# The second layer's adaLN weights summed on VectorE during the merge

## The chip, the cores and the metric

One core of a Trainium2 chip runs the whole program in one launch. The metric is the device time of an execution in microseconds. The engines are TensorE (matmuls, PE in the profile), VectorE (DVE), ScalarE (ACT), GpSimd (POOL) and SyncE (SP), which here only issues DMAs.

## What is computed

A block with a three-branch token mixer and an expert layer is followed by two transformer layers. Before each layer a conditioning vector makes the six modulation vectors (adaLN), and the change is about these:

```python
# first block (D_MODEL = 1024, SEQ = 256)
mod_l = jnp.split((jax.nn.silu(c) @ ada_w[l] + ada_b[l])[:, None, :], 6, axis=-1)
mod_c = jnp.split((jax.nn.silu(c_ctx) @ ada_w[l] + ada_b[l])[None, None, :], 6, axis=-1)
zc = modulate(rmsnorm(ctx, norm1_w[l]), mod_c[0], mod_c[1]) @ w_in[l] + b_in[l]
zl = modulate(rmsnorm(x, norm1_w[l]), mod_l[0], mod_l[1]) @ w_in[l] + b_in[l]
ml_c, st_f, st_b = mlstm_branch(zc[...], ...)       # context first, its state goes on
ml_l, _, _ = mlstm_branch(zl[...], ..., st_f, st_b)
x = x + mod_l[2] * token_mixer_out(zl, lat_grid, lp, ml_l)   # hyena, fnet, mLSTM, gated and merged
x = x + mod_l[5] * hier_moe(modulate(rmsnorm(x, norm2_w[l]), mod_l[3], mod_l[4]), lp)
...
# second block, for each of two layers
mod = jnp.einsum('bd,dn->bn', c_act, w_ada[layer]) + b_ada[layer]
sh1, sc1, gt1, sh2, sc2, gt2 = jnp.split(mod, 6, axis=-1)
```

Each modulation is a vector of 1024 times a matrix of 1024 by 6144, in float32. The kernel calls 512 columns of such a matrix a unit (2.10 MB): `ada0` is the first block's matrix, `ada1` that of the second block's first layer, `ada2` that of its second.

## The kernel before

**Stages.** The first 280 us project the input in ten passes (`PASSES`: q, k, kc, v, vc, o, vh, x1, x2, fn; kc and vc are the context's). A pass (`in_pass`) is four pieces of TensorE work on one weight unit, and between the pieces stand other jobs: the Hyena filters, the spectra, from pass 5 on the mLSTM's gates, and in passes 6 to 9 the heads. Head j needs, in turn, TensorE's row maximum, VectorE's weight arguments, ScalarE's exponential, VectorE's products and TensorE's values, and then `head_out` on VectorE, which frees the bank for the next head. The merge follows (280 to 457 us): twelve steps of gates and branch product on TensorE, sigmoid on ScalarE, `merge` on VectorE, with the Fourier and Hyena branches between them. Then come the output projection, the turn of x2 (normalised rows transposed), the router and the expert stage.

**Where the adaLN work stands.** 24 units, `ada0` 0 to 11 and `ada1` 0 to 11, are numbered 0 to 23. The first four are done ahead of the passes. Each pass has two of the other twenty, a after piece 0 and b after piece 2. A unit goes one of two ways. TensorE adds it to a bank with the 8 instructions of `strip_rows` (16 records in the trace, shape 20x512). Or, for those in `SUMMED` (10 to 14, 17, 19), VectorE's `ada_sum` multiplies and adds its eight blocks in place and `strip_columns` turns the row of sums with 16 one-column products. The last strip unit, 23 in pass 9, closes the bank: ScalarE copies it (`strip_in`) and `strip_columns` turns it.

**What sets the order.** Every engine's instructions are in written order. Weights pass through one ring of 18432 columns, cut in four quads during the passes and in three slots from the merge on. `unit_order` lists the loads and the releases, `unit_plan` gives each load its place and the release that it waits for. SP issues the loads in list order, and a load that waits holds all those behind it. `SUMS_BEFORE` names the loads that also wait for a count of VectorE's sums.

**Names for the prediction.** `norm_of_filters` is TensorE's first use of the context's hT, in pass 1. The wait at the end of pass 5 is that of `gate_columns`. In the merge `hyena_products(o)` on VectorE stands between `hyena_spectrum(o)` and `hyena_inverse(o)` on TensorE. `gates_of(n)` needs merge unit n // 2: gates 4 need unit 2, gates 10 unit 5.

## Time and profile before

| | us |
|---|---|
| median of 3 timed runs | 1922.56 (1921.06 to 1926.6) |
| the profiled execution | 1927.68 |
| its span | 1925.8 |
| TensorE busy | 1842.1, 96% |
| VectorE busy | 688.6, 36% |
| ScalarE busy | 312.8, 16% |
| mean granted TensorE clock | 0.989 of full |

The span runs from the first to the last instruction. Busy shares are means over the program. "idle before" in a row is the time for which an engine stood still ahead of it, with the engine that ended the wait; "records" are the lines that the trace has for an instruction (a float32 matmul of full rows leaves two).

### The profile page before, as it was taken

How to read it: one execution, taken by the hardware profiler on the slowest of the kernel's cores; microseconds unless marked ns; L12 is line 12 of the kernel's file. 1: busy time of each engine (PE TensorE's matmuls, PEld its weight loads, DVE VectorE, ACT ScalarE, POOL GpSimd, SP SyncE). 2: the span in 40 equal slices, each digit the busy share in tenths (PEclk: the TensorE clock that was granted, in tenths of full speed). 3: DMA queues.
4: the chain of work that ended last, by engine and by line, in shares of the span. 5: the costliest groups of instructions: out<-in, count | busy, mean ns of one | idle time of the engine just before them, and what ended most of it. 6: DMA issues, size and time to landing. Idle time of an engine off the chain costs nothing.

```text
span 1925.8 us, 39004 instructions
## 1 busy us (share of the span) xinstructions
PE 1842.1 (96%) x17396; PEld 1080.7 (56%) x17396; DVE 688.6 (36%) x1670; ACT 312.8 (16%) x729; POOL 26.5 (1%) x41
## 2 busy tenths in 40 slices
PE   6999989999898899999999999999999999999997
PEld 2654767886777555577676555443444444343444
DVE  3766772622433665432323553311110111111023
ACT  3211121001233324200001242100000010000001
POOL 0100000000000000000000000100000000000000
PEclk9999999999999999999999999999999999999999
DMA  9967743353699443467675323799999999999995
GB/s 359 341 244 272 272 153 118 131 178 119 263 401 388 164 141 123 148 235 256 236 242 190 131 91 128 294 402 420 409 419 409 416 409 405 420 412 415 410 413 217
DMA packets 156047, 538.84 MB, mean 280 GB/s; under 512 B 10016, under 2 KB 34944, under 8 KB 121712
## 3 DMA queue, kind: packets, MB, share of 16 engines
q1 hardware_dynamic: 149360, 509.15, 68.7%
q0 software_dynamic: 3728, 17.58, 2.6%
q10 hardware_dynamic: 2784, 9.53, 1.3%
q8 instruction: 140, 2.29, 0.5%
q14 instruction: 35, 0.29, 0.0%
HBM read 527.18 MB, written 12.19 MB: 280 GB/s over the span
## 4 chain that ended last, share of the span: by engine, by line
PE 87%; DVE 6%; DMA 2%; issue 1%; DVEq 1%; ACT 1%; SPq 0%; POOL 0%; ACTq 0%; POOLq 0%
PE ps L1279 24%; PE ps L1315 12%; PE ps L1225 8%; PE ps L1513 8%; PE ps L1089 4%; PE ps L1207 4%; PE ps L1237 4%; PE ps L892 4%; PE ps L1291 3%; PE ps L1104 2%; PE ps L1333 2%; PE ps L757 2%; PE ps L699 1%; PE ps L1302 1%; DMA ring<-in_ada_w 1%
## 5 line engine op out<-in xcount | busy, mean ns | idle before, releaser
L1279 PE MATMUL ps<-ring,arena 128*32 128x512 f32 (+1 forms) x4608 | 459.1, 557 | 0.0
L1279 PEld LDWEIGHTS ps<-ring,arena 128*32 128x32 f32 x4608 | 148.9, 110 | 294.0 <-issue 288.2
L1315 PE MATMUL ps<-ring,arena 128*32 128x256 f32 x4224 | 232.2, 379 | 0.1
L1315 PEld LDWEIGHTS ps<-ring,arena 128*32 128x32 f32 x4224 | 139.4, 110 | 96.9 <-issue 12.4
L2862 DVE TENSOR_TENSOR arena<-arena,ps 128x256 f32<-128x256 f32 (+1 forms) x72 | 27.0, 375 | 390.8 <-ACT arena L1965 390.8
L1513 PE MATMUL ps<-ring,hT 128*128 128x512 f32 (+1 forms) x384 | 154.9, 554 | 1.1 <-DVE hT L2214 1.1
L1225 PE MATMUL ps<-hT,ring 128*128 128x256 f32 x704 | 153.8, 379 | 0.7 <-DVE hT L2214 0.7
L1225 PEld LDWEIGHTS ps<-hT,ring 128*128 128x128 f32 x704 | 133.6, 190 | 23.4 <-issue 5.7
L1513 PEld LDWEIGHTS ps<-ring,hT 128*128 128x128 f32 x384 | 69.1, 190 | 68.7 <-issue 66.8
L2758 DVE TENSOR_SCALAR arena<-ps,ga,mod 128x128 f32<-128x128 f32 (+1 forms) x64 | 20.8, 389 | 197.5 <-PE ps L1330 118.1
L1089 PE MATMUL ps<-hT,ring 128*128 128x256 f32 x384 | 86.6, 385 | 3.9 <-DMA ring<-in_w_branch 3.9
L1965 ACT ACTIVATE arena<-ps 128x256 f32<-128x256 f32 (+1 forms) x72 | 21.2, 367 | 421.9 <-PE ps L1279 421.9
L892 PE MATMUL ps<-hT,ring 128*128 128x256 f32 x384 | 88.1, 383 | 0.8 <-DVE hT L2214 0.8
L1089 PEld LDWEIGHTS ps<-hT,ring 128*128 128x128 f32 x384 | 73.8, 193 | 14.6 <-DMA ring<-in_w_branch 4.3
L892 PEld LDWEIGHTS ps<-hT,ring 128*128 128x128 f32 x384 | 71.5, 190 | 17.6 <-issue 6.6
L1237 PE MATMUL ps<-ring,arena 128*128 128x512 f32 x176 | 78.4, 596 | 0.0
L1291 PE MATMUL ps<-ring,arena 128*32 128x128 f32 x2048 | 61.9, 276 | 10.5 <-issue 10.2
L2184 DVE SCALAR_TENSOR_TENSOR arena<-ring,cact,arena 128x512 f32<-128x512 f32 x84 | 63.1, 751 | 6.6 <-issue 0.4
L1291 PEld LDWEIGHTS ps<-ring,arena 128*32 128x32 f32 x2048 | 57.3, 111 | 14.2 <-issue 11.8
L2292 DVE SCALAR_TENSOR_TENSOR grow<-arena,colv,grow 128x189 f32<-128x189 f32 (+2 forms) x160 | 62.1, 430 | 6.3 <-issue 0.4
L2705 DVE TENSOR_TENSOR arena<-arena,ps 128x256 f32<-128x256 f32 x22 | 9.3, 421 | 145.8 <-ACT arena L1907 145.8
L1923 ACT ACTIVATE arena<-ps,mod,ga 128x128 f32<-128x128 f32 (+1 forms) x64 | 23.2, 443 | 226.5 <-PE ps L1330 130.9
(426 smaller groups left out, 1805.8 us busy)
## 6 DMA issues: line engine op xcount, KB each, us to landing
ring<-in_gate_up SPq DMA_DIRECT2D x160, 1024.0 KB, 14.2
ring<-in_down SPq DMA_DIRECT2D x104, 1024.0 KB, 15.2
ring<-in_gate_up_last SPq DMA_DIRECT2D x64, 768.0 KB, 13.9
ring<-in_w_ada SPq DMA_DIRECT2D x48, 768.0 KB, 6.1
ring<-in_w_in SPq DMA_DIRECT2D x36, 768.0 KB, 7.8
ring<-in_ada_w SPq DMA_DIRECT2D x24, 768.0 KB, 7.8
ring<-in_w_ada SPq DMA_DIRECT2D x24, 512.0 KB, 7.1
ring<-in_w_in SPq DMA_DIRECT2D x12, 1024.0 KB, 7.5
```

The lines of the kernel that those rows point to most:

```text
L757: last = mm(ps[32 * g:32 * g + rows, 2, :], cstrip[:, k, at:at + rows], quads[:, s, k * 512:(k + 1) * 512], start=r == 0 and i <= 4, stop= ...
L892: last = mm(ps[:, half, (i % 2) * T:(i % 2 + 1) * T], quads[:, s, k * 512 + i * P:k * 512 + (i + 1) * P], src[:, k, :], start=k == 0, stop ...
L1089: last = mm(ps[:, 2 * (n % 2), i * T:(i + 1) * T], w512(s, k, m * P, P), hT[:, k, :], start=k == 0, stop=k == KD - 1)
L1207: last = mm(ps[:, 2 * b + half, :], src[:, k, b * P:(b + 1) * P], w512(slots_[half], k), start=k == 0, stop=k == KD - 1)
L1225: m_ = mm(ps[:, hb, i * cols:(i + 1) * cols], ring[:, s, o:o + P], src[:, k, :], start=k == 0, stop=k == KD - 1)
L1237: m_ = mm(ps[:, base + 2 * b + half, :], region(R_AT, 2, T)[:, hb, b * P:(b + 1) * P], ring[:, s, o:o + 512], start=first and hb == 0, sto ...
L1279: last = mm(ps[32 * q:32 * q + 32, base + t_, 0:2 * n], src[:, k, 32 * t_:32 * t_ + 32], w[:, q], start=k == 0, stop=k == KD - 1)
L1291: last = mm(ps[32 * q:32 * q + 32, bank, t_ * P:(t_ + 1) * P], src[:, k, 32 * t_:32 * t_ + 32], w[:, t_ // 2, q], start=k == 0 and t_ == 0 ...
L1315: last = mm(ps[32 * q:32 * q + 32, bank + t_ // 2, (t_ % 2) * 256:(t_ % 2 + 1) * 256], rows[:, t_, o:o + 32], cells[:, cell, r * D + q * 2 ...
L1513: last = mm(ps[:, b, 0:w], hT[:, k, b * P:(b + 1) * P], w512(entry[0], k, 0, w, w), start=k == 0, stop=k == KD - 1)
L2184: last = v.scalar_tensor_tensor(acc, w, cact[:, c + k:c + k + 1], acc, ALU.mult, ALU.add)
L2292: v.scalar_tensor_tensor(acc[:, a, ro, co], grids[a][:, ri, ci], tap(b, (dr + 1) * 3 + dc + 1), acc[:, a, ro, co], ALU.mult, ALU.add)
```

## The change

Eight units of `ada1` (15, 16, 18 to 23, `MOVED`) leave the passes. Their loads go into slot 2 of the ring during the merge, one after another, each waiting for the sum of the one before. VectorE sums them into the arena at eight places of the merge. The merge units use slots 0 and 1 alone, and the output projection's first unit takes slot 2. During the turn of x2, `moved_columns` turns all eight sums with 128 one-column products in place of six filler matmuls; VectorE copies them to `modn` after the router. The passes keep twelve units by `PASS_UNITS`: TensorE's strip groups are those of 4 to 9, the last closing the bank in pass 8, and VectorE sums 10 to 14 and 17 as before.

```diff
-SUMMED = (10, 11, 12, 13, 14, 17, 19)
-LAST_STRIP = 2 * NA - 1
+SUMMED = (10, 11, 12, 13, 14, 17)
+MOVED = (15, 16, 18, 19, 20, 21, 22, 23)
+N_SUMS = len(SUMMED) + len(MOVED)
+LAST_STRIP = 9
+PASS_UNITS = ((4, None), (5, None), (6, None), (10, 11), (12, 13), (14, None), (7, 17), (8, None), (None, 9), (None, None))
...
     for p, name in enumerate(PASSES):
-        a, b = ADA_UNITS[4 + 2 * p:6 + 2 * p]
+        a, b = ([ADA_UNITS[i]] if i else [] for i in PASS_UNITS[p])
...
-    return loads + rest, releases + rest
+    late = [ADA_UNITS[i] for i in MOVED]
+    queue = rest[0:2] + late[0:4] + rest[2:3] + late[4:5] + rest[3:5] + late[5:7] + rest[5:6] + late[7:8] + rest[6:8]
+    return loads + queue, releases + rest
...
-        if name in ("merge", "out1"):
-            s = wide % NS
-            wide, full[s] = wide + 1, full[s] + 1
+        if name in ("merge", "out1") or (name, j) in MOVED_UNITS:
+            s = j % 2 if name == "merge" else 2 - 2 * j if name == "out1" else 2
+            wide, full[s] = s + 1, full[s] + 1
...
+        if (name, j) in MOVED_UNITS:
+            SUMS_BEFORE[name, j] = MOVED_UNITS.index((name, j))
+            continue
+        if name == "out1" and j == 0:
+            SUMS_BEFORE[name, j] = len(MOVED)
...
+            def moved_columns():
+
+                pe.wait_ge(sem("ada_sum"), N_SUMS)
+                for n, (_, u) in enumerate(MOVED_UNITS):
+                    for m in range(4):
+                        last = mm_strips(ps[:, 1, 4 * u + m:4 * u + m + 1], region(R_KC + 512 * n + m * P, P), const("ones")[:, 0:1],
+                                         start=True, stop=True)
+                last.then_inc(sem("moved_mm"), 1)
...
-            turn("x2", fill=(0, 6))
+            turn("x2", between=moved_columns)
...
-                if h == 3:
+                if h == 2:
                     strip_in(LAST_STRIP)
...
-                if j in (0, 2):
-                    ada_sum(*ADA_UNITS[19 if j else 17])
+                if j == 0:
+                    ada_sum(*ADA_UNITS[17])
...
-            dve.wait_ge(used, USED["ada1"][NA - 1])
+            dve.wait_ge(used, USED["ada0"][9])
...
             conv_hy(6, 7, 10)
+            ada_sum(*MOVED_UNITS[0])
+            ada_sum(*MOVED_UNITS[1])
             merge(0)
+            ada_sum(*MOVED_UNITS[2])
             hyena_products(0)
             merge(1)
             merge(2)
+            ada_sum(*MOVED_UNITS[3])
             hyena_out(0)
...
             merge(5)
+            ada_sum(*MOVED_UNITS[4])
             hyena_out(1)
...
             merge(6)
+            ada_sum(*MOVED_UNITS[5])
             merge(7)
...
+            ada_sum(*MOVED_UNITS[6])
             merge(8)
...
+            ada_sum(*MOVED_UNITS[7])
             merge(9)
...
             router1()
+            dve.wait_ge(sem("moved_mm"), 1)
+            v.tensor_copy(modn[:, 12:20], ps[:, 1, 12:20])
+            v.tensor_copy(modn[:, 24:48], ps[:, 1, 24:48])
```

TensorE in pass 8 of the kernel before, from its first piece to the values of head 5 (20x512 is a strip group, 128x129 a head's values, 128x256 alone a row maximum):

```order
L892 MATMUL ps<-hT,ring 128x256 x8
L757 MATMUL ps<-ring,cstrip 20x512 x8
L965 MATMUL ps<-late,blob 128x256
L892 MATMUL ps<-hT,ring 128x256 x8
L990 MATMUL ps<-arena,xn 128x129 x7
L892 MATMUL ps<-hT,ring 128x256 x8
L757 MATMUL ps<-ring,cstrip 20x512 x8
L965 MATMUL ps<-late,blob 128x256
L892 MATMUL ps<-hT,ring 128x256 x8
L990 MATMUL ps<-arena,xn 128x129 x7
```

and the same pass of the changed kernel:

```order
L915 MATMUL ps<-hT,ring 128x256 x8
L988 MATMUL ps<-late,blob 128x256
L915 MATMUL ps<-hT,ring 128x256 x8
L1013 MATMUL ps<-arena,xn 128x129 x7
L915 MATMUL ps<-hT,ring 128x256 x8
L769 MATMUL ps<-ring,cstrip 20x512 x8
L988 MATMUL ps<-late,blob 128x256
L915 MATMUL ps<-hT,ring 128x256 x8
L711 MATMUL ps<-blob,ring 32x20 x16
L1013 MATMUL ps<-arena,xn 128x129 x7
```

The first strip group is gone. The second is that of unit 9, and it closes the bank, so the 16 column products (32x20) stand here; they stood at the end of pass 9 before.

SP's queue in the merge of the kernel before, from merge unit 2 (`in_w_in` and `in_w_branch` are a merge unit's):

```order
L568 DMA ring<-in_w_in 128x4x512 [waits units_used]
L568 DMA ring<-in_w_in 128x4x512
L570 DMA ring<-in_w_branch 128x4x512
L568 DMA ring<-in_w_in 128x4x512 [waits units_used]
L568 DMA ring<-in_w_in 128x4x512
L570 DMA ring<-in_w_branch 128x4x512
```

and of the changed kernel, from the fourth moved load (`in_w_ada`) to merge unit 3:

```order
L537 DMA ring<-in_w_ada 128x3x512 [waits units_used,ada_sum]
L537 DMA ring<-in_w_ada 128x3x512
L537 DMA ring<-in_w_ada 128x2x512
L580 DMA ring<-in_w_in 128x4x512 [waits units_used]
L580 DMA ring<-in_w_in 128x4x512
L582 DMA ring<-in_w_branch 128x4x512
L537 DMA ring<-in_w_ada 128x3x512 [waits units_used,ada_sum]
L537 DMA ring<-in_w_ada 128x3x512
L537 DMA ring<-in_w_ada 128x2x512
L580 DMA ring<-in_w_in 128x4x512 [waits units_used]
L580 DMA ring<-in_w_in 128x4x512
L582 DMA ring<-in_w_branch 128x4x512
```

Merge unit 2 now stands behind a load that waits for a sum of VectorE's, and so does merge unit 3.

VectorE between the convolution of the blocks 6 and 7 and the first spectrum's products, before (L2506 is merge step 0, L2517 the first product):

```order
L2296 SCALAR_TENSOR_TENSOR arena<-arena,colv,grow 128x256 x2
L2506 TENSOR_TENSOR late<-rowv,ps 128x512
L2517 TENSOR_TENSOR xn<-ps,arena 128x1024
L2518 TENSOR_TENSOR arena<-ps,arena 128x1024
L2519 TENSOR_TENSOR xn<-ps,arena 128x1024
```

and now:

```order
L2322 SCALAR_TENSOR_TENSOR arena<-arena,colv,grow 128x256 x2
L2207 TENSOR_SCALAR arena<-ring,cact 128x512
L2210 SCALAR_TENSOR_TENSOR arena<-ring,cact,arena 128x512 x7
L2207 TENSOR_SCALAR arena<-ring,cact 128x512
L2210 SCALAR_TENSOR_TENSOR arena<-ring,cact,arena 128x512 x7
L2532 TENSOR_TENSOR late<-rowv,ps 128x512
L2207 TENSOR_SCALAR arena<-ring,cact 128x512
L2210 SCALAR_TENSOR_TENSOR arena<-ring,cact,arena 128x512 x7
L2543 TENSOR_TENSOR xn<-ps,arena 128x1024
```

Two sums stand ahead of merge step 0 and a third ahead of the products.

## Rows read from the trace of the kernel before

**Rows 1.** The page's chain that ended last, share of the span by engine.

```profile
PE 87%; DVE 6%; DMA 2%; issue 1%; DVEq 1%; ACT 1%; SPq 0%; POOL 0%; ACTq 0%; POOLq 0%
```

**Rows 2.** Timeline, passes 0 to 4: start, us, engine, line, operation, [idle before].

```profile
64.45 1.91 PE L757 MATMUL ps<-ring,cstrip 128*20 128x512 f32 x16
...
66.29 3.72 PE L892 MATMUL ps<-hT,ring 128*128 128x256 f32 x16
...
77.46 1.90 DVE L2214 TENSOR_SCALAR late<-ps,gac,modc 128x256 f32<-128x256 f32 x4
...
80.64 1.92 PE L906 MATMUL ps<-arena,blob 128*32 128x512 f32 x16
...
114.80 1.38 DVE L2350 TENSOR_SCALAR grow<-arena,colv 128x256 f32<-128x256 f32 x4 [10.48 <-ACT arena L1806]
...
120.34 0.48 DVE L2181 TENSOR_SCALAR ring<-ring,cact 128x512 f32<-128x512 f32 x1
...
126.66 0.43 PE L699 MATMUL ps<-blob,ring 128*32 128x1 f32 x32 [1.19 <-DVE ring L2184]
```

**Rows 3.** Timeline of TensorE, end of pass 5 to the first gates.

```profile
179.74 0.46 PE L953 MATMUL ps<-blob,late 64*128 64x64 f32 x4 [0.95 <-DVE late L2401]
...
181.23 3.65 PE L977 MATMUL ps<-arena 128*128 128x256 f32 x8
...
228.07 1.80 PE L990 MATMUL ps<-arena,xn 128*128 128x129 f32 x14 [1.25 <-DVE arena L2439]
...
281.77 3.69 PE L1117 MATMUL ps<-blob,arena 128*128 128x256 f32 x16 [2.65 <-DVE arena L2441]
...
289.36 8.86 PE L1089 MATMUL ps<-hT,ring 128*128 128x256 f32 x32 [3.90 <-DMA ring<-in_w_branch]
```

**Rows 4.** Timeline of VectorE, the mLSTM heads and the convolution behind.

```profile
224.74 1.65 DVE L2421 TENSOR_SCALAR xn<-ps,gcol 128x256 f32<-128x256 f32 x4
...
267.67 0.69 DVE L2450 TENSOR_TENSOR xn<-xn,blob 128x512 f32<-128x512 f32 x1 [1.59 <-ACT xn L1819]
...
269.58 0.15 DVE L2429 TENSOR_SCALAR dn<-ps 128x2 f32<-128x2 f32 x1
...
296.99 0.88 DVE L2296 SCALAR_TENSOR_TENSOR arena<-arena,colv,grow 128x256 f32<-128x256 f32 x2
```

**Rows 5.** Timeline of VectorE and TensorE, the merge and the turn of x2.

```profile
332.43 1.22 DVE L2517 TENSOR_TENSOR xn<-ps,arena 128x1024 f32<-128x1024 f32 x1 [13.89 <-PE ps L1145]
...
338.59 1.23 DVE L2525 TENSOR_TENSOR xn<-xn,arena 128x1024 f32<-128x1024 f32 x1
...
346.04 7.09 PE L1155 MATMUL ps<-blob,xn 128*128 128x256 f32 x32
...
409.35 0.69 DVE L2508 TENSOR_TENSOR rowv<-rowv,ps 128x512 f32<-128x512 f32 x1 [5.59 <-PE ps L1104]
...
431.59 7.07 PE L1089 MATMUL ps<-hT,ring 128*128 128x256 f32 x32
...
489.75 1.09 PE L825 MATMUL ps<-blob,xn 128*128 128x128 f32 x8 [0.66 <-DVE xn L2225]
```

**Rows 6.** SP's timeline, a load's issue to landing (median), the chain of waits.

```profile
277.43 0.92 SPq L568 DMA_DIRECT2D ring<-in_w_in  x2
...
442.14 1.43 SPq L527 DMA_DIRECT2D ring<-in_w_out  x3
...
ring<-in_w_out SPq DMA_DIRECT2D x1, 512.0 KB, 7.2
...
149.83 6.99 DMA ring<-in_w_ada
```

**Rows 7.** Three stretches: us, each engine busy, TensorE's clock, DMA share, GB/s.

```profile
182.00:184.00 2.00, 2.00 (x7) 1.55 (x6) 1.00 (x3) 0.97 (x1) 0.00 (x0) 0.50 1.05 398
...
282.00:284.00 2.00, 2.00 (x10) 1.74 (x10) 1.76 (x5) 0.00 (x0) 0.00 (x0) 1.00 1.04 392
...
339.00:345.00 6.00, 6.00 (x30) 5.28 (x29) 2.55 (x6) 0.84 (x2) 0.00 (x0) 1.00 1.05 396
```

More of the change, by code:

```diff
@@ L210, in unit_order @@
     for p, name in enumerate(PASSES):
-        a, b = ADA_UNITS[4 + 2 * p:6 + 2 * p]
+        a, b = ([ADA_UNITS[i]] if i else [] for i in PASS_UNITS[p])
         unit = ("in1", IN1_UNIT[name])
-        loads = loads + ([unit] if unit not in loads else []) + [a, b]
+        loads = loads + ([unit] if unit not in loads else []) + a + b
         held = [unit] if name not in ("k", "v") else []
-        early = 5 + 2 * p not in SUMMED and 5 + 2 * p < LAST_STRIP
-        releases = releases + [a] + ([b] + held if early else held + [b])
+        releases = releases + a + held + b
     rest = [("merge", j) for j in range(6)] + [("out1", j) for j in range(2)]
-    return loads + rest, releases + rest
+    late = [ADA_UNITS[i] for i in MOVED]
+    queue = rest[0:2] + late[0:4] + rest[2:3] + late[4:5] + rest[3:5] + late[5:7] + rest[5:6] + late[7:8] + rest[6:8]
+    return loads + queue, releases + rest
+MOVED_UNITS = [ADA_UNITS[i] for i in MOVED]
 LOADS, RELEASES = unit_order()
```

21 lines of the change are left out of this document (14 added, 7 removed).

## The prediction

> **What bounds the kernel now.** I read the page's chain of waits first: TensorE carries 87% of it and VectorE 6% [rows 1]. A removed matmul is worth its time only where TensorE waits for nothing behind it, so next I read TensorE's timeline from 50 to 500 us for the idle notes in brackets, then VectorE's and SP's over the same stretch.
>
> In the passes of the first projection TensorE runs without a gap to 124 us; after that it waits for VectorE at several places [rows 2, 3]. At 281.77 it waits 2.65 us for VectorE's last head, and at 289.36 another 3.90 us for the first merge unit's transfer [rows 3]. In the merge it is VectorE that sits idle: 13.89 us ahead of 332.43, 5.59 us ahead of 409.35 [rows 5]. That is the room into which eight sums go.
>
> **Step 1, the strip groups.** A group for one unit (16 records, 20x512) takes 1.84 us from start to start, 64.45 to 66.29 [rows 2]. Seven of the 13 in the passes go: 12.9 us of TensorE. What each is worth depends on the wait behind it.
>
> Passes 0 to 2 lose one each, 5.5 us. The first runs into VectorE: the context's low half of hT is written by the group that starts at 77.46 and ends at 79.36 [rows 2], whose place is set by ScalarE's square root and a convolution, none of which the change moves. TensorE reaches its first use at 80.64 [rows 2] and can't do so before about 79.4. So 1.25 us of that group is kept and the two others are kept whole, because VectorE idles 10.48 us further on, until ScalarE's copy of the context's k [rows 2], and that copy moves with TensorE: 1.25 + 2 x 1.84 = **4.9 us**. The sum of unit 10, for which TensorE waits 1.19 us at 126.66, starts from the same copy and moves with it.
>
> Pass 5 loses one. Behind it TensorE waits 0.95 us at 179.74 [rows 3] for the end of a chain that alternates VectorE and ScalarE from the gate products in the same pass on, and does not contain the group. Value **0 us**; the wait grows to 2.8 us.
>
> In the heads three groups and VectorE's sum of unit 19 go. TensorE waits there for VectorE (1.25 us at 228.07, twice 0.41 later) [rows 3], so VectorE sets the end. In pass 7, without the sum, the weights for the next head start when TensorE's row maximum is in, about 222.85 instead of 224.74, and everything behind them on VectorE comes 1.9 us earlier [rows 4]. That hides TensorE's group in pass 8: it will wait about 2.2 us where it waited 0.41. In pass 9 the earlier first half lets ScalarE's exponential finish before VectorE asks, so the 1.59 us of idle at 267.67 goes; head 6 then starts when TensorE's values are there, at about 266.4 instead of 269.58 [rows 4]. What follows on VectorE is unchanged, so the wait at 281.77 ends **3.2 us** earlier.
>
> The first merge unit (3.15 MB) is issued at 277.43, after the last strip unit's release, and TensorE waits for it until 289.36 [rows 3, 6]. In the new plan it follows the release of pass 8's weights, over 20 us earlier. The **3.9 us** go. What is late next is head 7, already counted.
>
> So the merge stage begins 4.9 + 3.2 + 3.9 = 12.0 us earlier.
>
> **The clock.** After the gap at 179.74 the granted clock is 0.50 (1.2 GHz) and four scores take 3.65 us, twice their time [rows 3, 7]; after the 3.90 us gap the gates take 8.86 us against 7.07 at 431.59 [rows 3, 5]. A fall costs 1.8 us. After the 2.65 us gap the clock stayed 1.00 (2.4 GHz) [rows 7]. The new gap ahead of the Fourier columns is 3.7 us, like the one that cost a fall, so I keep one fall at the stage's start, as now. The new gaps in passes 8 and 9, 2.2 and 2.0 us, are shorter than the 2.65 that cost none: value 0, bounds 0 and 1.8 each, and the same for a longer fall after pass 5. The Trainium skill (TensorE: Matmul & The Clock Gate, What's actually happening) says that the slow clock is the default and that activity is what lifts it. Read against this change, each new gap would be paid twice; that is rival A.
>
> **Step 2, eight sums in the merge.** A sum takes 6.2 us on VectorE: it starts at 120.34 and TensorE has it at 126.66 [rows 2]; eight are 49.6 us. They cost nothing where they end before anyone asks for what stands behind them, and each waits for its own transfer. All use slot 2, so each load is issued only when the sum before it is done, and SP's queue is one stream: merge units 2 and 5 stand behind such loads. What counts is L, the time of a 2.10 MB unit from first issue to landing. The out-projection unit at 442.14 is alone; its last DMA is issued at 443.1 and takes 7.2 us: L = 8.1 [rows 6]. A unit of pass 4 with others behind it lands 6.99 us after its last issue at 149.83 and was begun 0.9 us before that: 7.9 [rows 6]. A merge unit behind such a load adds 3.15 MB at 396 GB/s, 8.0 us [rows 7].
>
> - VectorE ends the convolution at 297.87 - 8.1 = 289.8 [rows 4] (the 3.9 us of transfer wait is not its own) and sum 0 at 296.0. Sums 1 and 2 each cost L + 6.4, so sum 2 ends at 325.0. It stands ahead of the spectrum's products, which could start at 332.43 - 12.0 = 320.4 and take 7.4 us [rows 5]. TensorE's inverse gets them at 332.5 and asks at 346.04 - 12.0 = 334.0 [rows 5]. Hidden, 1.5 us to spare.
> - Merge unit 2 goes out behind load 3: 325.1 + 8.1 + 8.0 = 341.2. The gates that need it follow the inverse, at 353.0 - 12.0 = 341.0 [rows 5]. **Loss 0.2 us**.
> - Sum 3 ends with the inverse, at 341. Sum 4 ends 0.7 us after the second inverse, whose result nobody needs for 15 us. Hidden.
> - Sum 5 follows merge step 6 (409.35) [rows 5] and ends at 405.2. Load 6 goes out then and merge unit 5 behind it, whose slot is free at 407.7: landing 405.3 + 8.1 + 8.0 = 421.4. The gates ask at 431.59 - 12.0 + 0.2 = 419.8 [rows 5]. **Loss 1.6 us**.
> - Load 7 lands near 427 and sum 7 ends at 433. Then the out-projection's weights are issued; they land at 441, and three gate and branch products of 10.4 us each, from 419.8 on, come before they are needed. Hidden, 6 us or more.
>
> In L the loss is (3L - 24.1) + (L - 6.5) = 4L - 30.6: 1.8 us at 8.1, 1.0 at 7.9, 5.4 at 9.0, and never below 0.
>
> **Step 3, the turn of x2.** 128 one-column matmuls replace six fillers. The 16 at 126.66 take 0.43 us [rows 2], so 128 take 3.4 at most; six fillers, at the rate of the eight equal matmuls at 66.29, 2.8, and TensorE still waits 0.66 us behind them [rows 2, 5]. 0 us; if single columns keep the clock up less well, the router's short products behind pay up to 1.1. VectorE's two small copies behind the router stand where it waits for the norm weights: 0. From the first expert stage on the order is the old one.
>
> **Sum.** 12.0 - 1.8 = 10.2 us. The profiled execution took 1927.68 (span 1925.8), which makes 1917.5; it lies 5.1 us above the median of the timed runs, 1922.56, and 10.2 from that median is 1912.4.
>
> **Rivals.**
> A. The clock falls in the new gaps too. For: it fell at 180 after less than 1.3 us of idle. Against: it held after 2.65 and 1.25. Two falls of 1.8 on the path: 10.2 - 3.6 = 6.6, that is 1916.0. The Trainium skill's rule would give that time as well.
> B. Loads issued from an idle queue together with a merge unit, or beside GpSimd's fills, land later. With L from 9.2 to 10.6 the loss is 6 to 12 us, the gain under 5.8: about 1919.5. Against: both whole units above, 7.9 and 8.1.
> C. Slower. The same chain of sum, load, sum, with the merge units behind it in SP's queue, costs more than all of step 1 from L = 10.6 on; at 11.5 the loss is 15.4, the net 3.4: 1926.0. For: the merge unit at 277.43, with two behind it, took 11.9 us [rows 3, 6]. Against: it has one and a half times the bytes.
> D. More: the fall at the stage's start goes (1.8) and the merge loses nothing (1.8): 13.8 us, 1908.8.
>
> **How the numbers follow.** Forecast 0.62, A 0.13, B 0.12, C 0.07, D 0.06. Below 0.3%, 5.8 us, a measurement can't tell a change from none. Faster: forecast, D and most of A, 0.79. Same: B and the rest of A, 0.14. Slower: C, 0.07. The range runs from D to a loss of 5.4 (L = 9.0) with part of A's, 1908.5 to 1918.5; it leaves out most of B and C.
>
> **What would show it.** TensorE waits about 0.4 us at its first use of the context's hT, 2.8 us at the end of pass 5, 2 us in passes 8 and 9, 3.7 us ahead of the Fourier columns, and not at all for the first merge unit; fnet's rows start 12 us earlier; the first inverse doesn't wait; gates 4 wait 0.2 and gates 10 wait 1.6 us for a DMA. Wrong if the products start past 326.5 because of sum 2, if a transfer wait above 3 us stands in the merge, or if the clock shows 0.5 in pass 8 or 9.

## The result and the profile after

The changed kernel is slower: 1928.43 us median (16 runs, 1924.3 to 1934.6) against 1922.46 (16 runs, 1917.7 to 1927.8); ratio 1.0028, 95% interval 1.0018 to 1.0037. The forecast was 1912.4, faster by 10.2 us. The profiled execution has a span of 1931.6 us, where before it was 1925.8.

The page's chain of waits, the row that answers to [rows 1]:

```profile
PE 80%; DVE 8%; DMA 5%; issue 2%; DVEq 2%; ACT 2%; SPq 1%; ACTq 0%
```

TensorE fell from 87% to 80%, VectorE rose from 6% to 8% and transfers from 2% to 5%. So work was taken from TensorE, but waits came in its place. The readings below compare with these five rows of TensorE's timeline of the kernel before: the projection's first product, the fillers of pass 3, the Fourier rows, the output projection and the first expert product.

```profile
51.88 3.69 PE L892 MATMUL ps<-hT,ring 128*128 128x256 f32 x16 [0.83 <-DVE hT L2214]
...
124.02 1.46 PE L694 MATMUL ps<-blob 128*128 128x256 f32 x6
...
298.06 7.07 PE L1127 MATMUL ps<-blob,xn 128*128 128x256 f32 x32
...
457.89 27.73 PE L1207 MATMUL ps<-ring,late 128*128 128x512 f32 x64 [1.97 <-DVE late L2510]
...
510.30 5.45 PE L1291 MATMUL ps<-ring,arena 128*32 128x128 f32 x192 [0.33 <-DVE dn L2766]
```

Where the waits stand is in TensorE's timeline of the changed kernel (start us, us, engine, line, operation, operands, shapes, count, idle before and its releaser). It answers to [rows 2, 3, 5]; TensorE's lines are up to 23 higher than before.

```profile
50.30 3.69 PE L915 MATMUL ps<-hT,ring 128*128 128x256 f32 x16 [0.83 <-DVE hT L2240]
...
117.13 1.46 PE L706 MATMUL ps<-blob 128*128 128x256 f32 x6
...
172.72 0.69 PE L976 MATMUL ps<-blob,late 64*128 64x64 f32 x4 [2.99 <-DVE late L2427]
...
234.02 3.34 PE L1013 MATMUL ps<-arena,xn 128*128 128x129 f32 x14 [2.23 <-DVE arena L2467]
...
274.55 5.38 PE L1140 MATMUL ps<-blob,arena 128*128 128x256 f32 x16 [3.98 <-DVE arena L2467]
...
286.67 7.07 PE L1150 MATMUL ps<-blob,xn 128*128 128x256 f32 x32
...
342.76 7.17 PE L1112 MATMUL ps<-hT,ring 128*128 128x256 f32 x32 [1.01 <-DMA ring<-in_w_branch]
...
426.59 9.83 PE L1112 MATMUL ps<-hT,ring 128*128 128x256 f32 x32 [4.95 <-DMA ring<-in_w_branch]
...
455.31 25.16 PE L1230 MATMUL ps<-ring,late 128*128 128x512 f32 x58 [1.62 <-DVE late L2536]
...
483.85 2.00 PE L711 MATMUL ps<-blob,arena 128*32 128x1 f32 x219
490.87 0.71 PE L711 MATMUL ps<-blob,arena 128*32 128x1 f32 x37 [5.03 <-issue]
...
512.74 5.45 PE L1314 MATMUL ps<-ring,arena 128*32 128x128 f32 x192 [0.33 <-DVE dn L2800]
```

Read it as a balance. The fillers of pass 3 moved from 124.02 to 117.13. The waits that the prediction named are there: 2.99 us (2.8 named), 2.23 (2.2), 1.67 us in pass 9 (2.0) and 3.98 (3.7), and none for the first merge unit. The Fourier rows, at 298.06 in the trace of before, are at 286.67, which is 11.4 us earlier. But the output projection, at 457.89 before, moved only to 455.31: the merge lost 8.8 us of them. Its rows show where: waits of 1.01 and 4.95 us for merge units, and gates at half clock behind the second (9.83 us for 7.07). And TensorE, in the 128 one-column products (two records each), stops for 5.03 us after 219 records, with "issue" as the releaser: the profile shows nothing that TensorE waits for. From the output projection's start to the first expert product it was 52.4 us (457.89 to 510.30), now it is 57.4 (455.31 to 512.74).

Now the chain of events ahead of gates 10. First, the waits that released each other between 380 and 430 us (start, us, what):

```profile
389.62 0.37 SPq L537
...
390.56 13.87 DMA ring<-in_w_ada
404.46 0.49 DVE arena L2207
...
410.76 0.37 SPq L537
...
412.24 0.71 SPq L580
...
413.58 12.96 DMA ring<-in_w_branch
...
426.59 3.78 PE ps L1112 x8
```

Load 5 is issued at 389.62, when sum 4 is done, and lands at 404.46: 14.8 us, where the prediction had L = 8.1 for a load. VectorE had been ready for sum 5 since 400.70 and waited 3.76 us. Sum 5 follows, then load 6, and merge unit 5 behind it in SP's queue at 412.24. Second, what the DMA engines carried meanwhile, from the DMA view of 385 to 412 us (a queue's packets, MB and share; an issue's median us to landing) and GpSimd's timeline:

```profile
q0 software_dynamic: 144, 3.28, 33.1%
...
sorted_moe<-in_x POOLq DMA_DIRECT2D x3, 11.2
```

```profile
393.51 1.55 POOL L653 DMA_DIRECT2D sorted_moe<-in_x  x3
```

GpSimd's three fills (they prepare the second expert stage's buffer), 3.28 MB from DRAM to DRAM, are issued 3.9 us behind load 5, while it is on its way.

Last, the granted clock in three stretches (us, each engine's busy time, clock, DMA share, GB/s): behind the waits of 2.99, 2.23 and 4.95 us a part of each stretch is at 1.2 GHz, the lower of the two levels. Behind the 3.98 us the Fourier columns take 5.38 us, and 3.69 in the kernel before.

```profile
176.00:180.00 4.00, 4.00 (x12) 3.19 (x11) 2.58 (x5) 1.06 (x1) 0.00 (x0) 0.57 0.23 89
234.00:240.00 6.00, 5.98 (x27) 5.68 (x28) 1.70 (x2) 0.00 (x0) 0.00 (x0) 0.72 0.00 0
426.00:436.00 10.00, 9.41 (x31) 7.87 (x32) 3.48 (x16) 0.00 (x0) 0.00 (x0) 0.70 0.58 208
```

### The profile page after: what moved, and what is told of

Same layout as the page of the kernel before. It is cut to its first block, busy times and chain, and to the rows that moved or that the text cites. A ratio compares the mean times of both kernels' runs of the same rounds, so it can differ in the third digit from the quotient of the medians.

```text
span 1931.6 us, 39319 instructions
## 1 busy us (share of the span) xinstructions
PE 1833.8 (95%) x17496; PEld 1083.7 (56%) x17496; DVE 728.3 (38%) x1728; ACT 312.6 (16%) x729; POOL 26.5 (1%) x41
## 4 chain that ended last, share of the span: by engine, by line
PE 80%; DVE 8%; DMA 5%; issue 2%; DVEq 2%; ACT 2%; SPq 1%; ACTq 0%
PE ps L1302 23%; PE ps L1338 11%; PE ps L1248 8%; PE ps L1536 8%; PE ps L1230 4%; PE ps L1260 4%; PE ps L915 4%; PE ps L1314 3%; PE ps L1112 2%; DMA ring<-in_w_ada 2%; PE ps L1356 2%; DMA ring<-in_w_branch 1%; DVE arena L2210 1%; PE ps L1325 1%; DMA ring<-in_ada_w 1%
## 5 line engine op out<-in xcount | busy, mean ns | idle before, releaser
L2210 DVE SCALAR_TENSOR_TENSOR arena<-ring,cact,arena 128x512 f32<-128x512 f32 x140 | 105.2, 751 | 11.5 <-issue 1.3
L1112 PEld LDWEIGHTS ps<-hT,ring 128*128 128x128 f32 x384 | 74.4, 195 | 17.2 <-DMA ring<-in_w_branch 6.8
```

What stands on the lines that cost most here:

```text
L1112: last = mm(ps[:, 2 * (n % 2), i * T:(i + 1) * T], w512(s, k, m * P, P), hT[:, k, :], start=k == 0, stop=k == KD - 1)
L2210: last = v.scalar_tensor_tensor(acc, w, cact[:, c + k:c + k + 1], acc, ALU.mult, ALU.add)
```

## The experiments

Three theories: **M**, the fills slow load 5 and with it the chain of sum, load and merge unit; **S**, TensorE runs out of instructions in the 128 short products, since they are done faster than new ones are supplied; **C**, the clock falls in the gaps that step 1 opens. This table has all runs. The two stretches are TensorE's, in the profiled execution: from the projection's first product to the output projection's first, and from there to the first expert product. The ratio is of timed runs to the kernel before, with its 95% interval. Each stretch is of one execution; e10 and e13, the same instructions in the same order, have ratios 0.0014 apart, so a difference of that size between two rows is not read on its own.

| kernel | to output proj. | to first expert | ratio | interval |
|---|---|---|---|---|
| before | 406.0 | 52.4 | 1 | |
| changed | 405.0 | 57.4 | 1.0028 | 1.0018 to 1.0037 |
| e1 no columns | 409.1 | 52.5 | 1.0003 | 0.9990 to 1.0015 |
| e2 first step alone | 394.9 | 52.5 | 0.9964 | 0.9954 to 0.9975 |
| e3 before + columns | 402.8 | 58.2 | 1.0042 | 1.0026 to 1.0057 |
| e4 32 wide columns | 407.9 | 60.4 | 1.0063 | 1.0040 to 1.0086 |
| e5 fills early | 396.6 | 58.1 | 1.0011 | 1.0000 to 1.0023 |
| e6 merge unit 5 first | 404.2 | 57.7 | 1.0048 | 1.0035 to 1.0062 |
| e7 fillers in gaps | 402.8 | 56.5 | 1.0026 | 1.0014 to 1.0038 |
| e8 columns earlier | 407.3 | 53.0 | 1.0037 | 1.0020 to 1.0054 |
| e9 rows for columns | 397.7 | 51.1 | 1.0016 | 1.0004 to 1.0028 |
| e10 combined | 396.7 | 51.2 | 0.9971 | 0.9959 to 0.9983 |
| e11 before + 64 columns | 402.4 | 52.4 | 1.0003 | 0.9991 to 1.0015 |
| e12 combined, no fillers | 396.6 | 51.3 | 0.9988 | 0.9977 to 0.9999 |
| e13 combined, copy moved | 394.8 | 51.1 | 0.9957 | 0.9945 to 0.9969 |
| e14 combined, 2 x 64 | 394.6 | 54.0 | 0.9972 | 0.9961 to 0.9984 |
| e15 before + fillers | 402.3 | 51.3 | 1.0007 | 0.9998 to 1.0015 |
| e16 e13 with half sums | 389.6 | 50.7 | 0.9928 | 0.9916 to 0.9941 |

### The change taken apart: e1, e2

e1:

```diff
-            turn("x2", between=moved_columns)
+            turn("x2", fill=(0, 6))
```

> The changed kernel with the 128 one-column products at the x2 turn, VectorE's wait for them and its two copies left out, and the six full-width fillers back in their place; the moved loads and the eight sums stay, but their results go nowhere (the second layer's adaLN columns of eight units are missing). Theory S (instruction supply): the 5.03 us in which TensorE stood with nothing to wait for, 37 products before the end of the 128, belong to this run of tiny products; without it the stretch from the output projection's start to the first product of L1291 goes from 57.4 us back to the kernel before's 52.4, and the time from 1928.4 to about 1923.4. Rival R (the ring's loads or the merge's order make TensorE stand there, whatever it runs): a stall of about 5 us stays in the turn, the time stays within 1 us of 1928.4.

The second stretch is back at 52.5 us and the ratio fell by 0.0025, 4.8 us. S was right on both. The profiled execution itself was the longest of its kernel (1935.7, median 1924.3): load 5 took 19.0 us there (391.60 to 410.59) and gates 10 waited 9.40.

e2 has neither the eight moved loads nor their sums and columns:

```diff
-    return loads + queue, releases + rest
+    return loads + rest, releases + rest
```

> Step 1 of the change alone: the passes run with the eight units gone, and the eight units are neither loaded nor summed anywhere (their adaLN columns are missing), the merge's units rotate over three slots and the six fillers are back. Theory: the passes and heads give what the changed trace shows at the Fourier rows, 286.7 against 298.1 us, of which 1.6 us is an earlier start-up, and nothing of it is lost again behind: 1922.5 - 9.8 = about 1912.7. What the clock takes in the new gaps (1.3 in pass 5, 1.5 in pass 8, 1.7 at the Fourier columns) is in that. Rival: the shorter passes bring the merge's loads against a wait of their own (the fills of GpSimd, a load of 2.1 MB not there), then the merge keeps a new wait and the time is 1915 to 1918.

1915.8 us, by the ratio 7 below before, not 9.8 or 10. The time is one that the rival named, but no merge unit is waited for, so the rival's mechanism is absent. TensorE's waits in e2 that tell:

```profile
233.81 1.80 PE L1010 MATMUL ps<-arena,xn 128*128 128x129 f32 x14 [2.22 <-DVE arena L2464]
...
272.73 6.24 PE L1137 MATMUL ps<-blob,arena 128*128 128x256 f32 x16 [4.00 <-DVE arena L2464]
```

The Fourier columns take 6.24 us for 3.69. Behind pass 5's wait, from the gate columns to the next strip group, e2 takes 9.54 us; e3, in whose profiled execution the clock doesn't fall there, takes 6.87. That is about 5.2 us of clock in e2. The first stretch is 394.9 us against 406.0 in the profiled execution of before; but in three other executions of the same code (e3, e11, e15 differ from before only behind or at the end of that stretch) it is 402.3 to 402.8. The profiled execution that the sum was made against had two clock falls on this stretch, 3.2 us by the Fourier rows against e3, that such a run need not have. So step 1 is worth 7.4 to 7.9 us here, and the timed 7 agree. By ratios, the change is: step 1, -0.0036; moved loads and sums, +0.0039 (e1 against e2); columns, +0.0025.

### The stop in the turn: e3, e4, e8, e11

e3, the kernel before with the columns:

```diff
-            turn("x2", fill=(0, 6))
+                for n in range(8):
+                    for m in range(4):
+                        mm_strips(ps[:, 1, 4 * n + m:4 * n + m + 1], region(R_KC + 512 * (n % 2) + m * P, P), const("ones")[:, 0:1],
+                                  start=True, stop=True)
...
+            turn("x2", between=columns_alone)
```

> The kernel before with one edit: the six full-width fillers at the x2 turn are replaced by 128 one-column products (of the same form as the changed kernel's, on columns that nobody reads). Theory S: TensorE stops for about 5 us inside the 128 with nothing to wait for, the first product of L1291 comes about 5 us later, the time goes from 1922.5 to about 1927.5. Rival R: the stop needs the changed kernel's other loads and sums ahead of it; here the 128 products hide in the wait for the normed rows as the six fillers do, and the time stays within 1 us of 1922.5.

TensorE's timeline of e3:

```profile
478.69 1.86 PE L699 MATMUL ps<-blob,arena 128*32 128x1 f32 x202
486.25 0.92 PE L699 MATMUL ps<-blob,arena 128*32 128x1 f32 x54 [5.70 <-issue]
```

The stop is there without any of the rest of the change, 5.70 us long, behind 202 records. The ratio is 1.0042, 8 us, more than the 5.8 of the stretch; the profiled execution was the fastest of its five, and where the other 2 us lie isn't shown. The rival is out.

e4, the same columns from 32 products of full width:

```diff
-                        last = mm_strips(ps[:, 1, 4 * u + m:4 * u + m + 1], region(R_KC + 512 * n + m * P, P), const("ones")[:, 0:1],
+                        last = mm(ps[:, 1, 4 * u + m:4 * u + m + 1], region(R_KC + 512 * n + m * P, P), const("ones")[:, 0:1],
```

> The changed kernel with the same columns from 32 products of 128x128 by one column in place of 128 products of 128x32: the same result in a quarter of the instructions. Theory S: the stop grows with the number of instructions; with a quarter of them it is 0 to 1.3 us and the time falls by 4 to 5 us to about 1924. Rival F (instructions are fetched at this place of the program in either kernel, and whatever stands there stops for it): the stop stays near 5 us, the time within 1 us of 1928.4.

```profile
487.09 10.84 PE L778 MATMUL ps<-blob,arena 128*128 128x1 f32 x64
```

```profile
487.00:490.00 3.00, 3.00 (x30) 3.00 (x29) 1.27 (x4) 1.44 (x3) 0.00 (x0) 1.00 0.89 325
494.00:498.00 4.00, 4.00 (x20) 4.00 (x20) 0.00 (x0) 0.00 (x0) 0.00 (x0) 0.50 0.79 328
```

There is no stop, as S says; yet the time is the worst of all. Each record now takes a weight load of 128x128 for a single column: 30 in 3.00 us at full clock, 20 in 4.00 us at half. 64 of them are 6.4 us at best, and the clock fell under them. I had counted instructions and forgotten what each costs. (The records of the 128x32 products went at 9 ns each: 219 in 2.00 us.) In the second stretch that makes 3.0 us against the changed kernel, while the ratio is 0.0035 higher, 6.7 us; in the profiled execution another 2.9 us are lost ahead of the output projection, where load 5 took 17.7 us.

e8, the 128 products at the end of the merge:

```diff
+            moved_columns()
             pe.wait_ge(sem("merged"), 12)
             out_proj("out1", macc)
-            turn("x2", between=moved_columns)
+            turn("x2", fill=(0, 6))
```

> The changed kernel with the same 128 one-column products moved ahead: from the x2 turn, where the ring's loads for the first MoE keep the DMA busy, to the end of the merge, ahead of TensorE's wait for the last merged half (about 454 us, DMA share 0 to 0.6), with VectorE's copies behind its last merge; the six fillers are back in the turn. Theory S in its form S1 (TensorE stops since its instructions come by DMA and stand behind the ring's loads): there is no stop, or one under 1 us, the products hide in the 1.62 us wait but for about 1 us, the stretch from the output projection to L1302's first product is 52.4 us, the time falls by about 4 us to 1924.5. Form S2 (so many short instructions outrun their supply whatever the DMA does): a stop of 2 to 5 us appears at the new place; the time stays within 2 us of 1928.4.

```profile
450.21 1.53 PE L711 MATMUL ps<-blob,arena 128*32 128x1 f32 x163
454.11 0.95 PE L711 MATMUL ps<-blob,arena 128*32 128x1 f32 x93 [2.37 <-issue]
```

The stop moved with the products and shrank to 2.37 us. From 450.21 to the output projection at 454.98 are 4.8 us where there was a wait of 1.62. So form S2 holds as to place: the stop comes with the products wherever they stand. Whether the ring's loads make it longer is open. At this place the DMA share was 0.47 up to the stop and 0.85 within it, and the stop took 2.37 us; in the turn it was 0.89 to 0.96 within the stop in five executions, and the stop took 3.85 to 5.70. That it is a wait for instructions is an inference: the profile names no releaser, and the count of short records decides (e4, e11 and e9 have no stop). The DMA view of the stop in the changed kernel, 485.8 to 490.9 us, shows what else lands in it:

```profile
q1 hardware_dynamic: 251, 1.86, 94.2%
q8 instruction: 1, 0.02, 1.1%
q14 instruction: 1, 0.01, 0.4%
```

Packets of kind "instruction" come by the same DMA engines, among 251 of the ring's. The profile's page counts 141 and 36 packets of that kind in two queues during the run, so in this trace instructions go on coming. That these two packets are the ones TensorE waits for isn't shown, only that they land in the stop.

e11, the kernel before with 64 such products (e3's edit with `for n in range(4)`):

> The kernel before with 64 one-column products in place of the six fillers at the x2 turn (128 of them gave a stop of 5.70 us after about 200 of their 256 records). Theory S with a store ahead of TensorE that holds what came before the burst: 64 products (128 records) come to an end before the stop, there is none or one under 1 us, the stretch is 52.4 to 53.4 us and the time within 2 us of before. Rival T (the stop comes at a place in the program, whose next piece is late whatever precedes it): a stop of 2 us or more appears in or behind the 64, the time is 2 to 5 us above before.

```profile
481.75 1.25 PE L699 MATMUL ps<-blob,arena 128*32 128x1 f32 x128
485.07 1.09 PE L832 MATMUL ps<-blob,xn 128*128 128x128 f32 x8 [2.08 <-DVE xn L2232]
```

No stop: TensorE is through in 1.25 us and waits for VectorE. The ratio is 1.0003. So the length of the run decides: 128 records in a row go through where 256 don't.

### The merge: e5, e6

e5:

```diff
+            pool.wait_ge(sem("hy_u"), 1)
+            for name in ("moe2",):
...
+                    pool.dma_start(sorted_of[name][r0:r1, :], A["x"][0, 0:r1 - r0, :]).then_inc(sem(f"{name}_sorted"), 16)
             pool.wait_ge(sem("hy_u"), 3)
...
-            for name in ("moe2",):
...
-                    pool.dma_start(sorted_of[name][r0:r1, :], A["x"][0, 0:r1 - r0, :]).then_inc(sem(f"{name}_sorted"), 16)
```

> The changed kernel with one edit: GpSimd's three fills of the second MoE's buffer (3.2 MB, DRAM to DRAM) start when hy_u is 1 (in the last mLSTM head, about 260 us) in place of 3 (about 392 us). Theory M (the fills slow the moved load 5, which takes 14.8 us from issue to landing where a lone one takes 8.0, and behind its sum stand load 6 and merge unit 5 in SP's queue): load 5 lands in about 8 us, sums 5 to 7 move up by up to 6.8 us, merge unit 5 is issued when its slot comes free (409) and TensorE's wait at gates 10 falls from 4.95 to under 1.5 us, and the half clock behind it (9.83 us for products that take 7.07) goes with it: the time falls by 5 to 7.7 us, to about 1922. Rival V (what costs is the volume, 16.8 MB more in the merge, wherever the fills stand): gates 10 still waits 3 us or more, or the same time is waited elsewhere in the merge, and the time stays within 2 us of 1928.4.

SP's and TensorE's timelines of e5:

```profile
388.00 18.72 SPq L537 DMA_DIRECT2D ring<-in_w_ada  x6
407.91 0.95 SPq L580 DMA_DIRECT2D ring<-in_w_in  x2
```

```profile
421.31 7.17 PE L1113 MATMUL ps<-hT,ring 128*128 128x256 f32 x32 [1.28 <-DMA ring<-in_w_branch]
...
447.37 27.73 PE L1231 MATMUL ps<-ring,late 128*128 128x512 f32 x64 [1.62 <-DVE late L2537]
```

Sum 5 doesn't wait for its load, merge unit 5 is issued when its slot is free, gates 10 wait 1.28 us and run at full clock; the stretch is 8.4 us shorter, 7.4 of it behind the Fourier rows. The timed gain is smaller than the 5 to 7.7 us expected: 1928.4 to 1925.1, or 0.0017 in the ratio.

Theory M is shown, but not as one number. With the fills in their old place load 5 took 12.2, 12.3, 14.8, 17.2, 17.7, 17.8 and 19.0 us in seven profiled executions (e9, e6, changed, e8, e4, e7, e1), and sum 5 waited for it in every one. With the fills early sum 5 waited in none of six (e5, e10, e12, e13, e14, e16). In e9, whose merge is the changed kernel's, gates 10 waited only 2.48 us, and from the Fourier rows to the output projection it took 162.5 us (168.6 in the changed kernel, 161.3 in e5):

```profile
419.18 7.17 PE L1120 MATMUL ps<-hT,ring 128*128 128x256 f32 x32 [2.48 <-DMA ring<-in_w_branch]
```

So the 8.4 us are the difference of two executions. What the fills cost on the median is the timed 0.0017 here and 0.0028 between e9 and e12, which differ by the same edit. Why the same fills slow the load by so different amounts isn't shown.

e6, the queue's order:

```diff
-    queue = rest[0:2] + late[0:4] + rest[2:3] + late[4:5] + rest[3:5] + late[5:7] + rest[5:6] + late[7:8] + rest[6:8]
+    queue = rest[0:2] + late[0:4] + rest[2:3] + late[4:5] + rest[3:5] + late[5:6] + rest[5:6] + late[6:8] + rest[6:8]
```

> The changed kernel with one edit in SP's queue: merge unit 5 stands ahead of moved load 6 in place of behind it. Theory M: the unit is then issued when its slot comes free, about 409.4 in place of 412.2, and lands alone, so the wait at gates 10 falls from 4.95 to about 1 us and the half clock behind it goes (2.8 us); but loads 6 and 7 and their sums come 5 to 8 us later, out_w's first half is issued at about 446 in place of 440 and is there by 454, in time for the output projection at 450 to 455 or up to 3 us late: the time falls by 3 to 7 us, to 1921 to 1925. Rival Q (the queue's order doesn't matter, the load of fills, sum 5 and unit 5 are limited by the DMA's rate): the wait at gates 10 stays over 3 us or moves whole to the output projection, the time stays within 2 us of 1928.4.

```profile
421.25 0.49 DVE L2207 TENSOR_SCALAR arena<-ring,cact 128x512 f32<-128x512 f32 x1 [14.06 <-DMA ring<-in_w_ada]
```

```profile
443.31 6.26 PE L1127 MATMUL ps<-arena,ring 128*128 128x256 f32 x16 [6.29 <-DVE late L2536]
```

Slower, against both. Gates 10 no longer wait, but VectorE now waits 14.06 us for load 6, its merge steps stand behind that sum, and TensorE waits 6.29 us for them. I had looked only at who needs the sum, not at what stands behind it on VectorE.

### The clock: e7, e15

e7, with `busy` (full-width products that nobody reads) ahead of four waits (gate columns, the values of passes 8 and 9, Fourier columns):

```diff
+                busy(5, 3, T)
                 pe.wait_ge(sem("ml_ready"), 3)
...
+                if j in (4, 6):
+                    busy(4 if j == 4 else 3, 3, T)
                 pe.wait_ge(sem("ml_p"), j + 1)
...
+                busy(7, 6)
                 pe.wait_ge(sem("z_in"), n_act)
                 pe.wait_ge(sem("ml_h"), 8)
```

> The changed kernel with fillers of TensorE put into four of the gaps that step 1 opened: 2.4 us before the gate columns of pass 5 (wait 2.99), 1.95 and 1.46 us before the values of passes 8 and 9 (waits 2.23 and 1.67), 3.4 us before the Fourier columns (wait 3.98). Theory C (the gaps are idle time that costs nothing by itself, but the granted clock falls to half behind three of them, at 183, 245 and 286 us of the trace, which costs 1.3, 1.5 and 1.7 us): the three falls go, TensorE reaches the merge's first gates about 4.5 us earlier, the time falls by 3 to 4.5 us, to about 1924.5. Rival W (the next wait is set by VectorE or a load, and takes back what the clock gives): the clock stays up, but gates 0 or the Fourier rows begin within 1.5 us of 279.8 and 286.7, the time stays within 1.5 us of 1928.4.

```profile
268.73 3.69 PE L1144 MATMUL ps<-blob,arena 128*128 128x256 f32 x16 [0.94 <-DVE arena L2471]
...
336.88 7.17 PE L1115 MATMUL ps<-hT,ring 128*128 128x256 f32 x32 [2.65 <-DMA ring<-in_w_branch]
...
424.07 8.90 PE L1115 MATMUL ps<-hT,ring 128*128 128x256 f32 x32 [8.30 <-DMA ring<-in_w_branch]
```

The clock stays up, the Fourier columns take 3.69 us and start 4.6 us earlier after the projection's start (219.6 against 224.3), the Fourier rows 6.3; then gates 4 and 10 wait 2.65 and 8.30 us for their loads, and the time is unchanged. C's mechanism is right and its gain was waited out, as W said of the time, though W looked for the wait ahead of the Fourier rows, not behind them. Gates 4 show it: 1.6 us more than in the changed kernel. The 8.30 us are not the fillers' alone, since load 5 took 17.8 us in this execution.

e15, the control, is the kernel before with `busy(5, 6)` ahead of its Fourier columns:

> The kernel before with 2.4 us of fillers ahead of its wait of 2.65 us for the Fourier columns, its largest gap in this stretch. If the combined kernel's gain were the fillers' alone, this would be 3 us or more faster than before. Theory: the gap's half clock (3.4 us of it at 300 in one profiled execution, none in another) costs 0 to 1.8 us, and the fall at the merge's first wait (3.8 us for w_branch) stays, since the fillers bring TensorE to it earlier: 0 to 1.5 us faster, 1921 to 1922.5.

1.0007: fillers alone bring the kernel before nothing. Only its gap ahead of the Fourier columns had them.

### Together: e9, e10, e12, e13, e16, e14

e9 puts rows for the columns:

```diff
+                for n in range(8):
+                    q = n % 4
+                    last = mm(ps[32 * q:32 * q + 32, n // 4, :], const("ones")[:, 0:32], region(R_KC + 512 * n, 512), start=True, stop=True)
...
+                for g in range(2):
+                    for m in range(4):
+                        last = mm_strips(ps[:, 1, 16 * g + m:16 * g + m + 13:4], region(R_KC + 512 * g + m * P, P), ident[:, 0:P:32],
+                                         start=True, stop=True)
...
+            turn("x2", fill=(0, 2), between=moved_rows)
+            busy(2, 2)
             router("x2", 0)
+            moved_columns()
```

> The changed kernel with fewer instructions for the same eight columns: in the x2 turn 8 products of ones with a sum of 512 columns (a row in each quarter of two banks) in place of the 128 one-column products, with 2 fillers ahead; ScalarE copies the two banks; 32 products of four columns, where three fillers stood behind the router's, turn the rows. Theory S (the stop is the supply of so many short instructions): 40 products in place of 128 in two places, no stop; the stretch from the output projection to the first MoE's first expert product goes from 57.4 back to 52.4 to 53.4 us, the time falls by 4 to 5 us, to about 1924. Rival F (instructions run out at this place whatever stands there, as in the merge's end where the stop was still 2.37 us): a stop of over 2 us stays in the stretch and the time falls by less than 2.

In e9, e10 and e12 the router's scores are written over a quarter of ScalarE's copy before TensorE turns it, so some columns are not the reference's; instructions and order are those of e13, where the copy lies clear. There is no stop, the second stretch is 51.1 us. The ratio fell by 0.0012, less than I expected; between e5 and e12, which differ by the same edit, it is 0.0023.

e10 has e5's, e7's and e9's edits, e12 e5's and e9's, e13 is e10 with the copy moved:

> The changed kernel with the three cures together: the fills early, the fillers of TensorE in the four gaps, the rows in place of the 128 products. Theory (M, C and S add, and C was taken back by M alone before): from the projection's first product to the output projection 396.6 us (the fills early) less 4.5 of the clock, and 52.5 behind it: the time is 1922.5 - 7.7 (step 1) - 3 to 4.5 (clock) + 1.7 (the merge's remaining waits) = 1911 to 1914. Rival W (the merge's chain of sum and load sets the end of the merge, so an earlier start is waited out): the fillers bring nothing beside e12, both at 1917 to 1919.

> The changed kernel with the fills early and the rows in place of the 128 products, without the fillers in the gaps. Theory: 1925.0 (the fills early alone) less the 5.0 to 5.8 of the stop: 1919 to 1920, 2 to 4 us below the kernel before. Rival: the stop was hidden in part by something else that comes out now; 1922 or more.

> The combined kernel of e10 with ScalarE's copy of the rows 2048 elements further on, clear of the router's scores (in e9, e10 and e12 the scores are written over a quarter of it before TensorE reads it). Same instructions, same order: the time of e10, 1917.8 within 1.5 us, 4 to 7 us below the kernel before in the same call.

e13 takes 1915.4 us (1913.4 to 1917.4) against 1923.2: ratio 0.9957, 8 us below before and 13 below the changed kernel. It leaves nothing of the reference out, and it beats both. e12 had 0.9988, 1919.3 us, as forecast. e10 had 0.9971, 1917.8 us, above its forecast and where its rival W put it; e13, which should have taken the same within 1.5 us, took 2.4 less. So in the combined kernel the fillers bring 0.0017 to 0.0031, and not nothing, as in e7; but e10's profiled execution still has one fall behind pass 5. TensorE's waits in e13:

```profile
339.17 7.17 PE L1124 MATMUL ps<-hT,ring 128*128 128x256 f32 x32 [2.29 <-DMA ring<-in_w_branch]
...
420.42 7.17 PE L1124 MATMUL ps<-hT,ring 128*128 128x256 f32 x32 [2.36 <-DMA ring<-in_w_branch]
```

Two waits for merge units remain. e16 tells what is behind them:

```diff
-                for k in range(KD):
+                for k in range(KD // 2 if moved else KD):
```

> The kernel of e13 with the eight moved sums over 4 of their 8 slices (the other half of each sum is left out): 3.1 us in place of 6.2 of VectorE each, the loads the same. Theory W (in the merge a chain of load, 8.0 us, and sum, 6.2 us, runs over the one ring slot and ends last at gates 4 and 10, 2.39 and 2.45 us in e10): both waits go, the stretch from the projection's first product to the output projection falls from 396.7 us by 4 to 5, the time by as much against e13. Rival D (the loads alone fill the DMA and end last): the waits stay over 1.5 us each and the time is within 1.5 us of e13.

Both waits are gone and the output projection's row has only its usual wait; the stretch is 5.2 us shorter (394.8 to 389.6), the time 5.5:

```profile
437.02 27.73 PE L1243 MATMUL ps<-ring,late 128*128 128x512 f32 x64 [1.62 <-DVE late L2552]
```

So the chain of sum and load ends last in the merge, and an earlier start of the merge is waited out there in part.

e14 has two runs of 64 one-column products in place of e13's rows:

> The combined kernel with the eight columns by one-column products again, in two runs: 64 in the x2 turn, 64 behind the router's products, where VectorE's masks are waited for (3.76 us). Theory S (TensorE's store of instructions, filled while the long products run, holds about 200 records of such): no stop in either run, the stretch from the output projection to the first expert product is 52.4 to 53.4 us, the time that of e13 within 1.5 us. Rival N (it is the number altogether that has to be fetched): a stop of 2 us or more in the second run or in the transposes between, the time 2 to 5 us above e13.

```profile
483.00 1.20 PE L712 MATMUL ps<-blob,arena 128*32 128x1 f32 x123 [0.20 <-issue]
...
489.20 0.52 PE L712 MATMUL ps<-msk,blob 128*32 128x16 f32 x23 [0.96 <-issue]
```

Neither theory as it stood: the first run of 128 records has no stop, the second and the masks' products behind it have small ones of 0.20 and 0.96 us, the second stretch is 2.9 us above e13's and the time 2.9 above. Halving the run takes most of the stop away, but the second half is paid in part.

## Why the prediction was wrong

**Step 1, the strip groups: the path right, the clock mis-sized.** Passes 0 to 2 gave 5.3 us (72.14 us from the projection's first product to the row at 124.02 before, 66.83 now; 4.9 predicted), the waits in the heads are those named, and the first merge unit's wait is gone. Where the clock stays up on both sides, in e3 and in e7, the Fourier rows begin 242.96 and 230.07 us behind the projection's first product: 12.9 us, where the prediction had 12.0. What was mis-sized is the term for the clock. It was 0 for the new gaps, with one fall kept. In the changed kernel's profile it fell behind 2.99, 2.23 and 3.98 us of idle, in e2 behind the first and the last; against e7 that is 6.3 and 5.4 us at the Fourier rows. The same gap doesn't always cost: after 2.23 us the values took 3.34 us in the changed kernel and 1.80 after 2.22 in e2. Rival A's rule, that the slow clock is the default and activity lifts it (the Trainium skill, TensorE: Matmul & The Clock Gate, What's actually happening), came nearer than my reading of one row in which the clock had held.

**The sum's base.** 12.0 us was read off one execution of before that had two falls and a longer first stretch (406.0 us) than three other executions of that code (402.3 to 402.8). Against the profiled execution the new falls partly take the place of old ones; against a run without the old ones they are a loss in full. Timed, step 1 brought 7 us.

**Step 2, "Sum 5 follows merge step 6 and ends at 405.2": this step failed.** It let VectorE's order set sum 5 and had no term for load 5, which it took to be there in time. The loads that "4L - 30.6" does count were priced well: loads 1, 2 and 6 took 8.0, 8.0 and 7.7 us, and merge unit 5 behind load 6 came 15.8 us after that load's issue (410.8 to 426.5), as 8.1 + 8.0 says. But load 5 took 14.8 us, because GpSimd's fills start when the second hyena output is ready, 4 us behind its issue. VectorE was ready at 400.70, the load was there at 404.46, and sum 5 ended at 410.73. The profile of before had the fills in the same place (402.82), beside transfers that nobody waited for. The merge lost 8.8 us where 1.8 were forecast: gates 4 waited 1.0 us (0.2), gates 10 4.95 (1.6), and 2.8 are the half clock behind that wait, for which the sum had no term. Two of the prediction's own signs of being wrong came with it, a transfer wait above 3 us in the merge and the slow clock in pass 8. Rival B named this cause, with a chance of 0.12, but as a longer L for every load, and its time didn't include the turn.

**Step 3, "0 us, bounds 0 to 1.1": this step failed.** I multiplied the 16 products at 126.66 by eight. The 32 records there, or 128 in e11, go through without a stop; in 256 TensorE stops for 5.0 us. The bound from the nearest row was no bound, because the cost isn't proportional to the count. Timed, the columns cost 4.8 us, most of the 5.4 by which the ratio makes the changed kernel slower; without them (e1) it is 1.0003.

Added up in the profiled executions: 11.4 gained to the Fourier rows (1.6 of it an earlier start of the projection), 8.8 lost in the merge, 5.0 in the turn. Together the stretch up to the first expert product is 2.4 us longer, and the span 5.8. The first MoE's stage after that took 2.1 us more than before's and the rest of the program 1.2. But over the eighteen profiled executions here, with the same instructions there, that stage ran from 154.2 to 160.2 us, so no part of that is put on the change.

## What to carry to other kernels

Before putting a load into an idle stretch, list everything that any queue issues there, in the new time as well as in the old: a transfer that nobody waits for becomes a cost once a chain runs beside it. For a chain over one slot (load, sum, load), work out for each load how late it may come before the next link waits. Shorten a link before filling TensorE's gaps, or part of the gain is waited out. When a sum starts from one profiled execution, look for clock falls in it that other executions lack. Don't scale a short instruction's price from 16 to 128: count the instructions in a row, and turn rows in place of columns where that takes a third of them.

## What the runs showed of the hardware

- TensorE stops in a run of 256 very short records: 3.85 to 5.70 us in the turn (five executions), after 219 records of 9 ns each in the changed kernel, and 2.37 us after 163 at the end of the merge. In a run of 128 there was no stop in e11 and in e14's first run, and 0.20 us in e14's second.
- A 128x128 fp32 weight load with one column behind it takes 100 ns a record at 2.4 GHz and 200 at 1.2 (e4).
- The executions of one kernel spread together with their clock: of e4's six, the one with a mean granted clock of 0.989 took 1925.8 us, the five at 0.982 to 0.983 took 1935.9 to 1940.3.
- DRAM-to-DRAM fills of 3.28 MB beside a 2.10 MB load: the load took 12.2 to 19.0 us in seven executions, where loads 1, 2 and 6 of the changed kernel took 7.7 to 8.0.
